# A four-layer hybrid transformer on one core: softmax sums inverted three steps ahead, head loads and the first split reordered, part of the last update on GpSimd

## The reference, cut to what matters

```python
for layer in range(DEPTH):
    u = rms_norm(h, norm_g[layer, 0])
    u = mixer(u)                      # kinds by layer: nsa, sb, swa, nsa
    h = h + rms_norm(u, norm_g[layer, 1])
    u = conv_ffn(rms_norm(h, norm_g[layer, 2]), ...)
    h = h + rms_norm(u, norm_g[layer, 3])
```

```python
p = masked_softmax(q @ k.T * scale - slope * dist, mask)   # e / sum(e)
o = gate_cmp * o_cmp + gate_sel * (p_sel @ v_sel) + gate_win * (p_win @ v_win)
```

## Time and profile before

| | us |
|---|---|
| median of three runs | 2573.88 |
| the profiled execution, its own time | 2574.38 |
| its span, first to last instruction | 2572.6 |
| TensorE busy in the span | 2514.6 |
| VectorE busy | 1607.4 |
| ScalarE busy | 1184.5 |
| GpSimd busy | 467.3 |

### The profile page before, as it was taken

One profiled execution on the slowest core, in us unless ns is written; L12 is line 12 of the kernel. 1 busy time (PEld: TensorE's weight loads), 2 busy tenths in 40 slices (PEclk: granted clock), 3 DMA queues, 4 the chain that ended last, 5 costly groups with the idle time before them and its releaser, 6 DMA issues.

```text
span 2572.6 us, 38307 instructions
## 1 busy us (share of the span) xinstructions
PE 2514.6 (98%) x13336; PEld 2072.8 (81%) x13336; DVE 1607.4 (62%) x2773; ACT 1184.5 (46%) x2035; POOL 467.3 (18%) x514
## 2 busy tenths in 40 slices
PE   8999999999999999999999999999999999999997
PEld 6987778888788678888878878888779778788886
DVE  7598577664353847667256677664386884766733
ACT  4467554443232845444245554443254684544431
POOL 2035321110010612111010021110010552111100
PEclk9999999999999999999999999999999999999999
DMA  4410123333233023332321123333233002233331
GB/s 160 142 34 2 42 83 98 98 98 98 87 99 99 9 66 99 98 97 90 103 85 57 42 82 99 98 98 98 79 116 122 18 2 58 87 94 97 90 106 49
DMA packets 61909, 210.91 MB, mean 82 GB/s; under 512 B 8528, under 2 KB 10320, under 8 KB 61776
## 3 DMA queue, kind: packets, MB, share of 16 engines
q1 hardware_dynamic: 61776, 209.13, 26.3%
HBM read 207.01 MB, written 2.10 MB: 81 GB/s over the span
## 4 chain that ended last, share of the span: by engine, by line
PE 91%; DVE 5%; ACT 1%; issue 1%; POOL 1%; DMA 0%; DVEq 0%; SPq 0%; POOLq 0%; ACTq 0%
PE psum L305 21%; PE psum L306 21%; PE psum L307 21%; PE psum L1310 3%; PE psum L1331 3%; PE psum L928 2%; PE psum L930 2%; PE psum L929 2%; PE psum L333 2%; PE psum L335 2%; PE psum L339 2%; PE psum L1297 1%; PE psum L1296 1%; PE psum L1093 1%; DVE h L501 1%
## 5 line engine op out<-in xcount | busy, mean ns | idle before, releaser
L305 PE MATMUL psum<-xh,w_hi 128*128 128x512 f32 x1712 | 666.6, 389 | 0.0
L306 PE MATMUL psum<-xh,w_lo 128*128 128x512 f32 x1712 | 666.1, 389 | 0.0
L307 PE MATMUL psum<-xl,w_hi 128*128 128x512 f32 x1712 | 666.1, 389 | 0.0
L267 DVE TENSOR_TENSOR w_lo<-w_raw,w_hi 128x1024 fp32r<-128x1024 f32 x226 | 284.1, 1269 | 527.5 <-ACT w_hi L261 525.7
L261 ACT ACTIVATE w_hi<-w_raw 128x1024 fp32r<-128x1024 f32 x226 | 236.2, 1057 | 590.6 <-PE psum L307 464.8
L307 PEld LDWEIGHTS psum<-xl,w_hi 128*128 128x128 f32 x1712 | 321.3, 188 | 66.8
L305 PEld LDWEIGHTS psum<-xh,w_hi 128*128 128x128 f32 x1712 | 321.4, 188 | 66.6 <-issue 0.2
L306 PEld LDWEIGHTS psum<-xh,w_lo 128*128 128x128 f32 x1712 | 321.4, 188 | 66.4
L709 DVE TENSOR_TENSOR w_lo<-w_raw,w_hi 128x1024 fp32r<-128x1024 f32 x160 | 209.3, 1308 | 253.6 <-ACT w_hi L705 253.6
L680 POOL TENSOR_TENSOR cv<-cv 128x512 f32<-128x512 f32 x88 | 133.9, 1521 | 793.7 <-ACT cv L634 773.0
L705 ACT ACTIVATE w_hi<-w_raw 128x1024 fp32r<-128x1024 f32 x160 | 168.4, 1052 | 234.8 <-PE psum L307 234.7
(11 more groups left out here) (221 smaller groups left out, 4027.1 us busy)
## 6 DMA issues: line engine op xcount, KB each, us to landing
w_raw<-w_up SPq DMA_DIRECT2D x176, 512.0 KB, 3.6
w_raw<-w_down SPq DMA_DIRECT2D x88, 512.0 KB, 3.6
w_raw<-nsa_in SPq DMA_DIRECT2D x56, 512.0 KB, 4.3
w_raw<-sb_in SPq DMA_DIRECT2D x24, 512.0 KB, 3.7
w_raw<-nsa_out SPq DMA_DIRECT2D x16, 512.0 KB, 3.6
w_raw<-swa_in SPq DMA_DIRECT2D x10, 512.0 KB, 3.8
w_raw<-sb_out SPq DMA_DIRECT2D x8, 512.0 KB, 3.6
w_raw<-swa_out SPq DMA_DIRECT2D x8, 512.0 KB, 3.6
```

What stands on the lines that cost most here:

```text
L267: nc.vector.tensor_tensor(w_lo[:, u % RING, :], w_raw[:, u % RING, :], w_hi[:, u % RING, :].bitcast(F32), ALU.subtract).then_inc(split_don ...
L305: nc.tensor.matmul(bank(p, o), wh[:, k, o, :], xhi(k), start=(first and k == 0), stop=False)
L306: nc.tensor.matmul(bank(p, o), wl[:, k, o, :], xhi(k), start=False, stop=False)
L307: mm = nc.tensor.matmul(bank(p, o), wh[:, k, o, :], xlo(k), start=False, stop=(last and k == 1))
```

## The change

Three edits.

1. In the attention steps VectorE serves the sum of step t + 3 in step t, after `copy(t)` and `biased(t + 4)`, both halves together. Ahead of the loop, `window_keys` comes before the second sum, and the third sum is made before the loop.
2. At the head SP issues the first quarter of the state, then `norm_g`, the first weight unit, `ident`, and the rest as before. ScalarE makes both `high` chunks of a pair and splits the weight unit before it squares them.
3. At the end ScalarE multiplies chunks 0, 1 and 2 of `ffn_u` by the norm factor in advance, GpSimd multiplies them by `rn` and adds them to the state, and VectorE does chunks 4, 5, 6, 7, 3. SP sends the chunks out in the order 4, 0, 5, 6, 1, 7, 3, 2.

```diff
+        LAST_V, LAST_G = (4, 5, 6, 7, 3), (0, 1, 2)
+
+        def act_last(act, s, u, g_post):
+            act.wait_ge(u_done, 4 * (s + 1))
+            for c in LAST_G:
+                nc.scalar.activation(u[:, c, :], u[:, c, :], ACT.Copy, scale=norm_g[:, g_post, c:c + 1]).then_inc(ug_done, 1)
+
+        def pool_last(pool, s, u):
+            pool.wait_ge(r_done, 2 * s + 2)
+            for k, c in enumerate(LAST_G):
+                pool.wait_ge(ug_done, k + 1)
+                nc.gpsimd.tensor_tensor(u[:, c, :], u[:, c, :], rn[:], ALU.mult).then_inc(ur_done, 1)
+                pool.wait_ge(ur_done, k + 1)
+                nc.gpsimd.tensor_tensor(h[:, c, :], h[:, c, :], u[:, c, :], ALU.add).then_inc(hp_done, 1)
...
-                for c in range(DC):
-                    if c >= 2:
-                        dve.wait_ge(h_done, 8 * s + c - 1)
+                for c in LAST_V:
                     update(c)
...
                     high(c)
-                    square(c, c)
                     if c % 2:
                         split_hi(act, c // 2)
+                        square(c - 1, c - 1)
+                        square(c, c)
...
             split_his(act, d0 + FC // 2 + 2, FC // 2 - 2)
+            if l == len(kinds) - 1:
+                act_last(act, s, ffn_u, 4 * l + 3)
             act_squares(act, s, 1, plan.down_p[l] + 1, d0 + FC)
...
-            for t in range(2):
-                floor(t)
-                inverse(t)
+            floor(0)
+            inverse(0)
             window_keys()
+            floor(1)
+            inverse(1)
             biased(2)
             biased(3)
+            floor(2)
+            inverse(2)
             for t in range(STEPS):
                 it, x = t // 16, t % 16
-                i = step_of(t)[3]
-                if i == 0:
+                if step_of(t)[3] != 1:
                     copy(t)
-                if t + 2 < STEPS:
-                    floor(t + 2)
-                if i >= 2:
-                    copy(t)
-                if t + 2 < STEPS:
-                    inverse(t + 2)
                 if t + 4 < STEPS:
                     biased(t + 4)
+                if t + 3 < STEPS:
+                    floor(t + 3)
+                    inverse(t + 3)
...
-            sp.dma_start(norm_g[:], ins["norm_g"]).then_inc(consts_landed, 16)
-            sp.dma_start(ident[:], ins["ident"]).then_inc(consts_landed, 16)
             for k in range(DC // 2):
                 sp.dma_start(h[:, 2 * k:2 * k + 2, :], ins["x"][:, 2 * k:2 * k + 2, :]).then_inc(x_landed[k], 16)
+                if k == 0:
+                    sp.dma_start(norm_g[:], ins["norm_g"]).then_inc(consts_landed, 16)
                 if k < AHEAD:
                     load_unit(sp, ins[kinds[0] + "_in" if kinds[0] else "w_up"][k], k)
+                if k == 0:
+                    sp.dma_start(ident[:], ins["ident"]).then_inc(consts_landed, 16)
...
-            for c in range(DC):
-                sp.wait_ge(h_done, 8 * last + c + 1)
+            for c in (4, 0, 5, 6, 1, 7, 3, 2):
+                if c in LAST_V:
+                    sp.wait_ge(h_done, 8 * last + LAST_V.index(c) + 1)
+                else:
+                    sp.wait_ge(hp_done, LAST_G.index(c) + 1)
                 sp.dma_start(out[:, c, :], h[:, c, :]).then_inc(out_landed, 16)
```

More of the change, by code:

```diff
@@ L197, in hybrid_layers @@
         h_done = sem("h_done")
+        ug_done = sem("ug_done")
+        ur_done = sem("ur_done")
+        hp_done = sem("hp_done")
         hs_done = sem("hs_done")
@@ L504, in dve_update @@
                 dve.wait_ge(r_done, 2 * s + 2)
-                for c in range(DC):
-                    if c >= 2:
-                        dve.wait_ge(h_done, 8 * s + c - 1)
+                for c in LAST_V:
                     update(c)
-                dve.wait_ge(h_done, 8 * s + DC)
+                dve.wait_ge(h_done, 8 * s + len(LAST_V))
                 dve.sem_inc(evac_v, 1)
@@ L2343, in _ @@
                 pool_sum_squares(pool, ch, s)
-                if not last:
+                if last:
+                    pool_last(pool, s, ffn_u)
+                else:
                     pool_h_squares(pool, s)
```

## The result

The changed kernel takes 2581.96 us (median of 11 executions, 2579.3 to 2583.4) against 2574.04 for the kernel before on the same chip (11 executions, 2572.28 to 2576.24): ratio 1.0029, 95% interval 1.0020 to 1.0037. It is 7.9 us slower; the forecast was +1.5 us, in a range that ended at 2580.0. The profiled execution took 2582.42 us with a span of 2580.6, 8.0 more than before. In the file after, lines behind the change have moved: `copy` L1440 is L1459, `floor` L1461 is L1480, `transposes` L1310 is L1329, `exps` L1376 is L1395, `dve_query` L1363 is L1382, `high` L543 is L559.

The account below looks back on a forecast made before the run. The prediction took TensorE as the bound, 91% of the end-determining chain. Edit 1 +3.9 (-1.8 - 2.2 + 9.0 - 1.1), edit 2 -0.7 and edit 3 -1.7 gave +1.5 us, 2575.4 on the median, range 2565.5 to 2580.

Parts of the forecast that it names:

- Start of the steps: Ahead of each layer's attention loop: moving window_keys shortens TensorE's wait before scores(2); net -0.9 us for each layer.
- The later steps: Attention steps: copy(t + 1) waits behind the floor; stalls after x = 14, 10 and 2, 9.0 us for two layers.
- rival B: Attention steps: every step with i = 1 stalls, not only those with extra work; about 9 us, 2584; chance 0.15.
- rival A: Later attention steps do not stall, as ScalarE's work slides into the room or the bank is free; 2565.8 us; chance 0.24.
- the first group: First group of a layer's attention steps: beyond the start and the query of x = 10, no loss was priced.
- step 12: Attention step 12: floor(12) made one step ahead removes TensorE's 1.13 us wait; -1.1 us in each layer.
- Edit 2: Head: ident lands at 6.0, ScalarE starts 0.4 us later, two squares leave the path to the first w_hi; -0.7 us.
- the pessimistic bound: Head: ident lands as late as the first weight unit did, making the head's change +0.2 us.
- the two squares: Head: two ScalarE squares leave the path to the first w_hi, some 1.1 us.
- Edit 3: Tail: VectorE does five chunks, GpSimd three; last work near 2568 us; -1.7 us, bounds -2.7 and 0.
- Clock: TensorE's drop to 1.2 GHz at 2010 us goes with the shorter start wait; -1.1 us, bounds 0 and -1.7.
- Rival C: Layer boundaries: shifted work changes which waits trip the clock; 1.7 us a drop, 2573.7 or 2577.1; no separate chance.

Follow-up runs that it names:

- e11_three_spread: Edit 1 alone (sums three steps ahead) with part of window_low moved from the first group to earlier groups' x = 5 and 6; median 1.3 us below edit 1 alone.
- e5_extras_first: Edit 1 alone on the kernel before, with VectorE's extra work (window_low, dve_query, low) ahead of floor(t + 3) in every step; +1.51 us over before, interval holds zero.
- e8_copy_first: Edit 1 alone on the kernel before, but in steps with i = 1 copy(t + 1) comes ahead of floor(t + 3) and inverse(t + 3); -0.55 us, interval holds zero.
- e9_ident: Edit 2 alone on the kernel before, with ident on its own semaphore, on which only TensorE waits; -1.10 us, interval holds zero.
- e10_spread: Kernel before with window_keys ahead of the second sum, sums two steps ahead, window_low spread over groups; six executions average 2567.9 us, four 2569.8.

## Why the prediction was wrong

- **Start of the steps: right in kind.** Forecast -0.9 for each layer, TensorE's wait 1.61 to 0.4. Measured 0.37, and -0.9 net in layer 0: -1.24 at `scores(2)`, +0.35 at the first interval, where I had 0.3.
- **The later steps: right.** Forecast stalls of 0.8, 0.4 and 0.3 us after x = 14, 10 and 2, 4.5 for a layer. Measured +0.92, +0.48 and +0.20, 4.8 for a layer. The row arithmetic had `copy(31)` 0.94 us behind the floor; it was 1.01. The feared condition of rival B, a stall also at x = 6, did not come in the later groups (1.87, 1.35 and 2.32 stay), and rival A's sliding in did not either. (Rival B's 9 us is 0.3 us at 32 places; with the 18 that it names beside them it would be 15.)
- **The step that failed: the first group.** I counted stalls "in three groups" and gave the first only its gain, "-1.1 in each layer" at step 12, though rival B mentions that "the first group also carries `window_low`". The rows say +0.59 at x = 4, +0.2 to 0.3 at x = 5, 8 and 9, +0.16 at x = 1, and step 12 gained 0.6, not 1.1, because its floor still came at 183.68 behind that backlog. Apart from the start's 0.35 that is +0.8 for a layer where the sum had -1.1: 3.9 us in both, of the 6.4 missed. The cause is `window_low` behind the wait for the exponentials: e11_three_spread takes away the stalls from x = 5 on and the late step 12, e5_extras_first and e8_copy_first the one of x = 4. The 0.16 at x = 1 stays in all of them and is not explained.
- **Edit 2: wrong sign.** Forecast -0.7, by `ident` landing at 6.0. It landed at 2.14 + 5.0 = 7.1, the pessimistic bound; I had let the whole stream move by the 0.93 us, but the first unit landed at 1.68 + 5.2 = 6.9 as before. Measured +0.3 at the first matmul, +1.05 in the time (the interval holds zero): up to 1.75 of the miss. On the two profiled executions the two squares gave 1.0 (w_hi's copy starts 1.24 instead of 2.28 us behind ScalarE's first work; forecast 1.1), and ScalarE's start took 1.5 where the sum had 0.4. e9_ident shows that `ident` was the gate: without it the first matmul comes 1.4 earlier.
- **Edit 3: right.** Forecast -1.7, measured -1.71 alone and -1.9 by rows. VectorE needed 8.66 us (forecast 9.1), GpSimd 8.06 (9.3): GpSimd was held up less than I had thought.
- **Clock.** The stretch at 2010 us went, as forecast, and cost 1.4, near the 1.1 taken. But taking one execution's rows for the kernel was a risk: of the five profiled kernels with the old start three lack that stretch, and the mean granted clock of before's executions runs from 0.994 to 0.998. Rival C's 1.7 us a stretch is 0.4 to 0.6 at a layer boundary, and their number there was two before and two after.
- **The parts together.** The span grew by 8.0, forecast 1.5. Of the 6.5 between, the first groups are 3.9, the head 2.5 (1.3 of it the longer half-pace phase of that execution), the later steps 0.6; the clock and the tail came out 0.3 and 0.2 better.
- **The range** gave "slower" 0.15 and ended at 2580.0, 2 us short. Each rival varied the later groups, which I had counted well; none varied the group that I had not counted.

## What to carry to other kernels

An in-order engine that is made to look further ahead waits in the place of whatever stands behind that wait; before moving an operation earlier, ask when its input is made, and put the work that others need ahead of it. Count every repetition of a loop that carries extra work; here the one left out was the first, which carried work for all the others. And look for what makes the late operation late: here moving other work out of its way gave more than doing it sooner, and one small constant behind a large load, on a shared semaphore, undid a reordered head.

## What the runs showed of the hardware

The length of TensorE's half-pace phase at the start differs between kernels with the same head. The 10 us stretches show PEclk 1.00 there, so it is read from the starts of the matmuls. From the first matmul to full pace it took 3.1 us in e8_copy_first and 6.0 in e11_three_spread, which share the head of before, and 6.1 after the change; the eight profiled kernels with the old head have 3.1 to 6.0, the five with edit 2's DMA order 4.3 to 6.1. In the timeline of TensorE after it ends here, where the distance of the starts falls from 0.43 to 0.26 and, behind these rows, 0.23:

```profile
16.15 0.63 PE L336 MATMUL psum<-xh,w_hi 128*128 128x512 f32 x1
16.57 0.60 PE L338 MATMUL psum<-xh,w_lo 128*128 128x512 f32 x1
17.00 0.42 PE L336 MATMUL psum<-xh,w_hi 128*128 128x512 f32 x1
17.26 0.40 PE L338 MATMUL psum<-xh,w_lo 128*128 128x512 f32 x1
```

So 1.3 of the 1.8 us by which the two profiled heads differ lies within what kernels with one and the same head show, and nothing here ties it to edit 2. The Trainium skill, TensorE: Matmul & The Clock Gate, Part 1, says that the cold phase varies from run to run of one kernel; the spread of 3.1 to 6.0 us fits, but each kernel here was profiled once, so no run shows it for one kernel. The granted clock inside the kernel does vary from execution to execution: of e10_spread's ten the six with a mean of 0.998 average 2567.9 us, the four with 0.996 or 0.997 average 2569.8. What decides at a layer boundary stays open: the wait there was the same 1.85 us in all kernels, and no run varied it.

GpSimd and VectorE do not always hold each other up. At the tail VectorE's four chunks from PSUM took 0.75 and 0.69 us for each operation beside a busy GpSimd, as before without it, and GpSimd's took 1.27; only where VectorE read SBUF alone did the two operations take 1.42 and 1.63, and GpSimd's 1.59. The Trainium skill, Perfetto Trace Analysis, Optimizing Scalar/DVE Operations, doubts that such offloading helps; here it saved 1.9 us, with an operand in PSUM in each operation of four of VectorE's five chunks. No run moved chunks to GpSimd while VectorE kept only operands in SBUF. In the steps a `floor` on 128x2 elements took 0.17 us, but 0.57 at 166.65, where GpSimd was working.
